# Modulation of a fused transformer kernel: feature-major tiles and one multiply-and-sum for each condition's column

## The reference

```python
for i in range(DEPTH):                       # 2 layers
    mx = (silu(c) @ w_mod[i] + b_mod[i]).reshape(B, 9, 1, D)     # for x
    mz = (silu(c_ctx) @ w_mod[i] + b_mod[i]).reshape(9, D)       # for z
    x = ffn_sublayer(x, mx, 0, ...)          # adaln_in(mod[0], mod[1]) ... gate mod[2]
    z = ffn_sublayer(z, mz, 0, ...)
    hx = adaln_in(x, g[2], mx[3], mx[4])     # rmsnorm(x, g) * (1 + scale) + shift
    yx = short_conv_mixer(hx, ...)           # layer 0; layer 1: window attention
    x = adaln_out(x, yx, g[3], mx[5], 1.0)   # x + weight * gate * rmsnorm(y, g)
    x = ffn_sublayer(x, mx, 6, ...)
```

## Time and profile before

| | us |
|---|---|
| median of 3 runs (2553.28 to 2557.42) | 2557.05 |
| the profiled execution, own time | 2558.84 |
| its span | 2557.5 |
| PE busy, 12614 matmuls | 2350.1 (92%) |
| DVE busy | 1600.0 (63%) |
| ACT busy | 900.6 (35%) |
| POOL busy | 176.5 (7%) |
| mean granted TensorE clock, share of 2.4 GHz | 0.925 |
| FFN 0, from its first matmul to its last | 60.85 to 450.88 |
| convolution | 483.00 to 672.39 |
| FFN 1 | 705.53 to 1096.01 |
| FFN 2 | 1128.12 to 1518.55 |

### The profile page before, as it was taken

The page is one execution under the profiler, slowest core; times in us unless marked ns, Lnnn a source line. Parts: engine busy times, 40 slices in busy tenths (PEclk is TensorE's granted clock), DMA queues, the critical chain, the costliest instruction groups (busy, mean ns, idle before and its releaser), DMA issues. The chain is left out here.

```text
span 2557.5 us, 32863 instructions
## 1 busy us (share of the span) xinstructions
PE 2350.1 (92%) x12614; PEld 1944.9 (76%) x12614; DVE 1600.0 (63%) x3977; ACT 900.6 (35%) x1542; POOL 176.5 (7%) x156
## 2 busy tenths in 40 slices
PE   5999999599699999959999987897997998999998
PEld 1788887488578888848888866577997975579998
DVE  6666668775676666876666685545455545445555
ACT  2322222422332222242222234455444444334444
POOL 2000001200300000120000022001002001001001
PEclk8999999799799999979999988898998996579999
DMA  7233434133123343413343332103556521014554
GB/s 275 99 120 144 152 133 155 58 148 114 74 99 144 133 160 123 149 74 133 127 153 148 124 140 87 42 25 113 177 179 211 184 86 50 1 67 149 182 173 140
DMA packets 62822, 322.45 MB, mean 126 GB/s; under 512 B 6446, under 2 KB 11182, under 8 KB 40778
## 3 DMA queue, kind: packets, MB, share of 16 engines
q1 hardware_dynamic: 60000, 314.33, 33.7%
q10 hardware_dynamic: 2666, 6.02, 0.7%
HBM read 319.27 MB, written 1.05 MB: 125 GB/s over the span
## 5 line engine op out<-in xcount | busy, mean ns | idle before, releaser
L418 PE MATMUL ps_g<-h,w_hi 128*128 128x512 f32 (+1 forms) x3360 | 963.1, 373 | 29.1 <-DVE h L788 28.7
L418 PEld LDWEIGHTS ps_g<-h,w_hi 128*128 128x128 f32 x3360 | 602.2, 191 | 150.5 <-DVE h L788 28.2
L746 DVE TENSOR_TENSOR w_lo<-w_raw,w_hi 128x1024 fp32r<-128x1024 f32 (+2 forms) x498 | 536.1, 1118 | 268.7 <-ACT w_hi L1187 267.1
L418 PE MATMUL ps_g<-h,w_lo 128*128 128x512 f32 (+1 forms) x1680 | 619.9, 369 | 0.0
L1187 ACT ACTIVATE w_hi<-w_raw 128x1024 fp32r<-128x1024 f32 (+2 forms) x498 | 455.4, 965 | 229.9 <-PE ps_g L418 202.9
L715 DVE SCALAR_TENSOR_TENSOR mod_acc<-mod_raw,cond,mod_acc 128x128 f32<-128x128 f32 x1792 | 489.3, 349 | 0.0
L418 PE MATMUL ps_g<-hid,w_hi 128*128 128x512 f32 (+1 forms) x1664 | 456.3, 362 | 1.5 <-DVE hid L944 0.9
L418 PEld LDWEIGHTS ps_g<-h,w_lo 128*128 128x128 f32 x1680 | 320.2, 191 | 56.5
L1272 ACT ACTIVATE gate_tmp<-ps_g 128x512 f32<-128x512 f32 (+1 forms) x118 | 61.1, 518 | 768.7 <-PE ps_g L418 768.7
L418 PEld LDWEIGHTS ps_g<-hid,w_hi 128*128 128x128 f32 x1664 | 293.3, 189 | 44.8 <-DVE hid L944 1.2
L418 PE MATMUL ps_g<-hid,w_lo 128*128 128x512 f32 (+1 forms) x832 | 298.3, 359 | 0.0
(11 more groups left out here) (235 smaller groups left out, 1986.6 us busy)
## 6 DMA issues: line engine op xcount, KB each, us to landing
w_raw<-in_gu SPq DMA_DIRECT2D x110, 1024.0 KB, 5.4
mod_raw<-in_w_mod SPq DMA_DIRECT2D x128, 512.0 KB, 3.4
w_raw<-in_conv_cu SPq DMA_DIRECT2D x8, 1024.0 KB, 5.5
w_raw<-in_w_in_a SPq DMA_DIRECT2D x8, 1024.0 KB, 4.7
w_raw<-in_w_in_d SPq DMA_DIRECT2D x8, 1024.0 KB, 4.8
w_mod<-in_w_mod SPq DMA_DIRECT2D x3, 2048.0 KB, 14.3
w_raw<-in_dn00a SPq DMA_DIRECT2D x8, 768.0 KB, 5.0
w_raw<-in_dn01a SPq DMA_DIRECT2D x8, 768.0 KB, 5.0
```

Of the source, the lines that this page charges most:

```text
L418: mm = pe.matmul(ps_g[:, 2 * (u % 2) + m, 0:T], w[wp][:, k, m * P:(m + 1) * P], acts[ap][:, k, 0:T], start=(k == 0 and n == 0), stop=(k == ...
L746: dve.tensor_tensor(w_lo[u % 2][:, cols], w_raw[u % 2][:, cols], w_hi[u % 2][:, cols].bitcast(F32), ALU.subtract).then_inc(lo_made, 1)
```

## The change

Tiles of w_mod are laid out with the 128 output features on the partitions and the 1024 inputs along the row. Both conditions, after silu, stand on every partition in a new tile `cond_b` (128 x 2 x 1024). For each condition, DVE multiplies the tile by the condition, sums along the row and adds the bias in one `tensor_tensor_reduce`, which leaves the finished column in `mod_sb`. Nothing is left for TensorE's partition sums and for `mod_keep`. The product itself is not needed: for the first condition it goes to PSUM (`dump`), for the second it overwrites the tile.

Ahead of unit 0 there are 16 tiles: eight scale tiles by TensorE in two groups of four, and eight shift tiles by DVE, from buffers of their own. The tiles on the way begin with 16 and belong to every unit of FFN 0, the convolution (now `conv_b` too), FFN 1 and the first 36 units of FFN 2. In the turn of u DVE makes tile MOD_OF[u] itself. `wide`, the input of the taps, has two buffers in place of eight, and the attention's scratch moves to other places.

```diff
-N_FIRST = 2 * NC + 1
+N_FIRST = 2 * NC
...
-MOD_OF = numbered(FFN_UNITS[0] + phase_units("conv_cu", "conv_out") + FFN_UNITS[1] + FFN_UNITS[2], N_FIRST)
-assert len(MOD_OF) + N_FIRST == N_MODS - 1
+MOD_OF = numbered((FFN_UNITS[0] + phase_units("conv_cu", "conv_b", "conv_out") + FFN_UNITS[1]
+                   + FFN_UNITS[2])[:N_MODS - N_FIRST], N_FIRST)
...
+    cond_b = sb("cond_b", [P, 2, D], F32, b1)
+    dump = ps_s[:, 2:4, :].rearrange("p a n -> p (a n)")
...
     def sync_program():
...
+        sp.dma_start(cond_b[:], t["cond"].partition_broadcast(P)).then_inc(cond_in, 16)
+        sp.dma_start(w_scale[0], t["w_scale"][0]).then_inc(scale_in[0], 16)
         sp.dma_start(x[:, :, 0:S], t["x"]).then_inc(x_in, 16)
+        shifts(0, 4)
         sp.dma_start(x[:, :, S:T2], t["ctx"]).then_inc(x_in, 16)
+        sp.dma_start(w_scale[1], t["w_scale"][1]).then_inc(scale_in[1], 16)
+        shifts(4, NC)
         for u, unit in enumerate(UNITS):
             if u >= 2:
                 sp.wait_ge(lo_made, 2 * (u - 2) + 2)
             sp.dma_start(w_raw[u % 2][:, 0:unit.elems], t[unit.src][unit.at]).then_inc(raw_in[u % 2], 16)
-            g = MOD_OF.get(u, 0)
...
-            if g > N_FIRST:
-                if g == N_FIRST + 1:
-                    sp.wait_ge(first_acc, STEPS * SUMMED)
-                else:
-                    sp.wait_ge(mod_step, STEPS * (g - N_FIRST - 1))
+            if u in MOD_OF:
+                g = MOD_OF[u]
+                if g >= N_FIRST + 2:
+                    sp.wait_ge(mod_step, 2 * (g - N_FIRST - 1))
                 sp.dma_start(mod_raw[g % 2][:], t["w_mod"][g]).then_inc(mod_in[g % 2], 16)
...
     def tensor_program():
         def feature_phase(name, acts, kc, mt, T, ready=None):
             for u in phase_units(name):
                 feature_unit(u, acts, kc, mt, T, ready if u == FIRST[name] else None)
-                if u in MOD_OF:
-                    mod_sum(MOD_OF[u])
...
     def vector_program():
+        def products(w, g, done, before):
+            for s in range(2):
+                if s == 0 and before:
+                    dve.wait_ge(done, before - 1)
+                dve.tensor_tensor_reduce(dump if s == 0 else w, w, cond_b[:, s, :], 1.0, b_mod[:, g, s:s + 1],
+                                         ALU.mult, ALU.add, mod_sb[:, g, s:s + 1]).then_inc(done, 1)
...
         def mod_products(g):
-            dve.wait_ge(mod_in[g % 2], ((g - N_FIRST - 1) // 2 + 1) * 16)
-            dve.wait_ge(mod_done, SUMMED + g - N_FIRST - 1)
-            accumulate(g % 2, mod_raw[g % 2][:], mod_step, STEPS * (g - N_FIRST))
+            n = g - N_FIRST
+            dve.wait_ge(mod_in[g % 2], 16 * (n // 2 + 1))
+            products(mod_raw[g % 2][:], g, mod_step, 2 * n)
...
-            if u in MOD_OF:
-                mod_keep(MOD_OF[u])
-                if not keep_off:
-                    mod_products(MOD_OF[u] + 1)
+            if u in MOD_OF and not keep_off:
+                mod_products(MOD_OF[u])
```

More of the change, by code:

```diff
@@ L133, in build @@
     tok = sb("tok", [P, 9])
-    mod_acc = sb("mod_acc", [P, 2, 2, P])
-    stats = mod_acc[:].rearrange("p a b n -> p (a b n)")[:, 0:5 * 64].rearrange("p (a n) -> p a n", n=64)
+    stats = sb("stats", [P, 5, 64])
     y = sb("y", [P, NC, T2])
-    mod_raw = [sb(f"mod_raw{j}", [P, NC, P]) for j in range(2)]
+    mod_raw = [sb(f"mod_raw{j}", [P, D]) for j in range(2)]
     mod_sb = sb("mod_sb", [P, N_MODS, 2])
@@ L146, in build @@
     h1 = [sb(f"h{j}", [P, NC, T2], F32R, b1) for j in range(2)]
[L147 removed]
+    wide = sb("wide", [P, 2, 2, S + 2], F32, b1)
+    cond_b = sb("cond_b", [P, 2, D], F32, b1)
     early1 = ExitStack()
[L149 to L150 removed]
+    w_scale = [y[:].rearrange("p a (b n) -> p (a b) n", n=P).rearrange("p (m k) n -> p m k n", m=4),
+               sb("w_scale", [P, 4, NC, P], F32, early1)[:]]
+    w_shift = sb("w_shift", [P, NC, D], F32, early1)
     early1.close()
+    apart = ExitStack()
+    sb("skip0", [P, NC, T2], F32, apart)
+    kv_raw = sb("kv_raw", [P, 8 * S], F32, apart)
+    sb("skip1", [P, NC, T2], F32, apart)
+    q_raw = sb("q_raw", [P, NC, S], F32, apart)
+    apart.close()
     hid1 = [sb(f"hid{j}", [P, FFN_HALVES[0], T2], F32R, b1) for j in range(2)]
@@ L282, in build @@
     stored = sem("stored")
-    w_mod_in = [sem(f"w_mod_in{j}") for j in range(6)]
+    cond_in = sem("cond_in")
+    scale_in = [sem(f"scale_in{j}") for j in range(2)]
+    shift_in = [sem(f"shift_in{j}") for j in range(NC)]
     raw_in = [sem(f"raw_in{j}") for j in range(2)]
@@ L364, in tensor_program @@
     def tensor_program():
[L365 to L373, removed]
         def first_mods():
@@ L720, in first_mods @@
             dve.wait_ge(consts_in, 48)
[L721 to L730, removed]
-                    w = w_mod[3][:, n] if n < 4 else mod_raw[0][:]
-                    accumulate(n % 2, w, first_acc, STEPS * n)
-                else:
-                    accumulate(n % 2, mod_raw[1][:], mod_step, 0)
-            dve.wait_ge(first_turned, 1)
-            dve.wait_ge(mod_done, SUMMED)
-            dve.tensor_tensor(mod_sb[:, 0:N_FIRST, :], ps_s[:, 2, 0:2 * N_FIRST].rearrange("p (m s) -> p m s", s=2),
-                              b_mod[:, 0:N_FIRST, :], ALU.add).then_inc(first_kept, 1)
-            dve.wait_ge(first_kept, 2)
+            dve.wait_ge(cond_made, 2)
+            for n in range(2):
+                for g in range(4 * n, 4 * n + 4):
+                    dve.wait_ge(shift_in[g], 16)
+                    products(w_shift[:, g, :], g, first_mod, 2 * g)
+                tiles = slice(NC + 4 * n, NC + 4 * n + 4)
+                dve.wait_ge(first_turned, n + 1)
+                dve.tensor_tensor(mod_sb[:, tiles, :], ps_g[:, 2 + n, 0:8].rearrange("p (m s) -> p m s", s=2),
+                                  b_mod[:, tiles, :], ALU.add).then_inc(first_kept, 1)
+            dve.wait_ge(first_kept, 3)
+            dve.wait_ge(first_mod, 2 * NC)
         def low_split(u):
@@ L1203, in first_mods @@
                            ACT.Silu).then_inc(cond_made, 1)
-            for n in range(3):
+            act.wait_ge(cond_in, 16)
+            act.activation(cond_b[:], cond_b[:], ACT.Silu).then_inc(cond_made, 1)
+            for n in range(2):
                 act.wait_ge(by_pe, n + 1)
-                act.activation(turn[0:2, n, :], ps_s[0:2, n % 2, :], ACT.Copy).then_inc(copied_by_pe, 1)
-                if n < 2:
+                act.activation(ring[n][0:2, :], ps_g[0:2, n, :], ACT.Copy).then_inc(copied_by_pe, 1)
+                if n == 0:
                     act.wait_ge(x_in, 32)
-                    for c in range(4 * n, 4 * n + 4):
+                    for c in range(NC):
                         square(sum_in(0), c, x[:, c, :], T2)
-                else:
-                    high_split(0)
-                    high_split(1)
+            high_split(0)
+            high_split(1)
             act.wait_ge(first_kept, 1)
```

100 lines of the change are left out of this document (31 added, 69 removed).

## The result

The changed kernel takes 2733.91 us (median of four runs, 2727.96 to 2739.45) where the kernel before takes 2555.75 beside it; the ratio is 1.0702, with a 95% interval of 1.0688 to 1.0715. It is slower by 7%. The forecast was 2720 with a range of 2640 to 2775. The profiled execution took 2727.96 (span 2726.6), which is the fastest of the four; the one of before took 2558.84.

A forecast was written before the change was run, and what follows sets the result against it. TensorE bounds the kernel before; after the change a one-turn loop through SP's wait would. FFNs +50, +54, +45, convolution +20, start -6 sum to +163 on 2558.84: 2722, taken as 2720 us, range 2640 to 2775.

The forecast's parts named there:

- The loop: SP's load, landing, split and products in one turn instead of two: 12.35 us per gu turn against TensorE's 11.15.
- The products: DVE's two new multiply-and-sums of 1024 columns per turn: 1.23 us a condition, 2.46 a turn.
- The upper bound of 2.9: Longest products per turn: two of 1225 ns, sum read not overlapped, 0.14 us each for writing the product.
- POOL's collision: In dn..b POOL's add falls on DVE's products and blocks them: 1.0 us added per turn.
- The convolution: Stage forecast from its loop turns: 209.8 us against 189.4, +20.
- FFN 0 and FFN 1: Stages slowed by the one-turn loop: +50 and +54 us, each with the later norm behind it.
- Ahead of unit 0: Start of the program, taken as bound by load arrivals: -6 us, between bounds of 2 and 10.
- The gaps: Behind FFN 0 and FFN 1 the norm starts 8.4 us later, as the last evacuation stands behind DVE's products.
- The one on the clock: Rival: TensorE's idling in dn..b drops its clock to 1.2 GHz, +74 us, 2795 in all; chance 0.08.
- The multiply-and-sum ran at full rate: Answers the rival of half rate with both operands in SBUF: 4.9 us a turn, 3005 in all; chance 0.04.
- The loop was not shorter than its rows: Answers the rival of a shorter loop that still binds: 2646 us; chance 0.10.
- The estimate from the Trainium skill: Tile and unit landing together as 2.0 us plus bytes over 436 GB/s: 5.6 us; sum 30 us lower.

## Why the prediction was right, and where it was off

**The loop** was the step that decided, and it holds: 12.35 us by the sum, 12.31 in the trace (median of 48 turns in gu); dn..a 10.5 and 10.38; a dn..a turn that splits a gu unit 11.75 and 11.66 to 11.98; dn..b with POOL 10.9 and 10.63; conv_cu 13.7 and 13.7; conv_b 12.9 and 12.9. Moving it a turn away gave back 238 us, and forcing it on the old kernel cost 436.

**The products** were put at 2.46 from rows with 512 and 256 columns and one operand in PSUM; they take 2.49 (114.59 to 117.08), the same with the product written to PSUM or to SBUF (1.29 and 1.28). The upper bound of 2.9 was not needed.

**POOL's collision** is there in dn..b, with 1.0 us. The product that it hits starts at 450.97 and takes 1.01 us longer, of the 1.21 that are left of POOL's add; the next is not slowed. By the Trainium skill, "SBUF — State Buffer", Summary: rules for kernel authors, a DVE operation with two SBUF inputs and a GpSimd one that reads SBUF block each other; the trace agrees. I had read this out of the earlier trace rows, where the operation of line 712 that is hit reads one tile and a column and not two tiles; only the rows after show it for two. In conv_out I counted one collision; there were two in two of its turns.

**The sizes that were off.** The convolution came out at +28.4, not +20.4. The term that was mis-sized is the end of it: I let the last unit start with its split, and did not see that the first unit of conv_out reads the last hidden tile, whose low half stands on DVE behind a split and therefore behind a landing. TensorE stops inside the unit (it began at 692.5):

```profile
706.48 1.22 PE L402 MATMUL ps_g<-hid,w_hi 128*128 128x512 f32 x2 [9.49 <-DVE hid L826]
...
702.92 2.36 DVE L709 TENSOR_TENSOR w_lo<-w_raw,w_hi 128x1024 fp32r<-128x1024 f32 x2 [5.80 <-ACT w_hi L1143]
705.20 1.22 DVE L826 TENSOR_TENSOR hid<-prod,hid 128x1024 fp32r<-128x1024 f32 x1
```

It then had the rest of that unit and three more to do at its own pace, to 748.79. With the hidden tile ahead of the split that wait of 9.49 is down to 1.41, and the convolution is 23.5 shorter.

FFN 0 and FFN 1 came out 4.6 and 2.8 us above the forecast (FFN 2 with its gap 2.5 below, as the dn..b turns were 0.3 shorter than my sum). Here it is the landing that was taken as constant. I used its median, and the median was right (5.46 to ACT's start in gu), but six of 59 there are 1.2 to 2.2 us late, and in the loop each of those is paid in full: 14 us in the three FFNs with those of the smaller units. One that took 7.1, in GB/s, the 8.5 us from 155 on in 40 slices; the second row is what came on the queue of instructions in the same 8.5 us (packets, MB, share):

```profile
GB/s 0 0 0 0 0 77 96 193 231 270 347 386 347 482 463 463 520 251 501 463 231 578 386 270 540 154 39 39 39 0 39 39 0 39 0 0 0 0 0 0
...
q8 instruction: 1, 0.02, 0.7%
...
w_raw<-in_gu SPq DMA_DIRECT2D x1, 1024.0 KB, 7.1
```

All but the last few packets are there after the usual time, and a tail of single packets (39 GB/s in a slice is one packet of 8 KB) comes up to 1.5 us later. The instruction queue brought one packet of 16 KB meanwhile, and that is the common case. In the FFNs of all ten traces, 123 of 137 late loads (over 0.8 us later than the median of their size) had such a packet beside them, and 113 of 983 of the others did; in the changed kernel they are 7 of 10 and 10 of 102 (112 of its 114 units there, all but the first two). So most late landings come with a fetch of instructions. How one packet holds up the others isn't shown, and three late loads of the changed kernel had none. With two turns of room a late landing costs nothing: the kernel before has 21, and its three FFNs take 390.0 to 390.5 us.

**Ahead of unit 0** it is -5.0 where I took -6. DVE's sixteen multiply-and-sums there end at 45.3. Five of them take 2.3 us instead of 1.3, while POOL adds. I had the arrivals as the bound. They were it only up to 31.09; from there the last eight run without a gap, so DVE and its collision with POOL set the end, which the forecast did not have. That the size came out near is in part luck. (The loads ran less evenly, too, than my 400 to 430 GB/s: the earlier trace rows have 347 to 378 in five slices.) The splits follow at 45.41 (50.42 before), and unit 0:

```profile
26.95 2.28 DVE L686 CUSTOM_DVE_ANT_0 w_shift<-w_shift,cond_b,vecs 128x1024 f32<-128x1024 f32 x1
...
45.41 4.63 DVE L709 TENSOR_TENSOR w_lo<-w_raw,w_hi 128x1024 fp32r<-128x1024 f32 x4
...
55.84 1.19 PE L402 MATMUL ps_g<-h,w_hi 128*128 128x512 f32 x2 [3.06 <-DVE h L746]
```

**The gaps** of +8.4 came out at +6.4 and +8.0: the last unit of dn0b was held up too, so the last addition (499.62 after a last matmul at 492.45) is 7.2 late and not 9.2. **The rest of the program** is 5.9 us shorter, 1000.9 against 1006.8. That is not told apart from the spread: in six other runs with the changed kernel's second block the same stretch takes 997.8 to 1005.1. No experiment was made on it.

**The rivals.** The one on the clock was partly true. Mean clocks of the FFNs are 0.96 to 0.97 against 1.00. This is where it goes (windows as above; the last row is of PE's timeline):

```profile
326.00:334.00 8.00, 8.00 (x36) 6.50 (x35) 1.31 (x3) 0.00 (x0) 0.00 (x0) 1.00 0.52 199
...
337.60:339.50 1.90, 1.87 (x4) 1.49 (x5) 1.90 (x4) 0.00 (x0) 0.00 (x0) 0.50 0.00 0
339.50:342.00 2.50, 2.50 (x10) 2.00 (x9) 1.69 (x3) 0.00 (x0) 0.00 (x0) 0.75 0.18 38
342.00:345.00 3.00, 3.00 (x15) 2.43 (x14) 0.00 (x0) 0.00 (x0) 0.00 (x0) 1.00 1.00 392
...
288.00:290.00 2.00, 2.00 (x9) 1.65 (x10) 2.00 (x3) 0.00 (x0) 0.00 (x0) 1.00 0.00 0
...
337.63 1.22 PE L402 MATMUL ps_g<-h,w_hi 128*128 128x512 f32 x2 [2.45 <-DVE w_lo L709]
```

TensorE works at 1.00 up to 335, waits 2.45 us for the split of unit 24, and resumes at 1.2 GHz (0.50); unit 24 takes 12.8 us in place of 11.4. After a wait of 3.1 us (284.9 to 288) it kept its clock. Fourteen units of the three FFNs are 1.3 to 2.6 us longer in this way, all behind a wait of 1.9 to 3.5 us, and six more are 0.8 to 2.0 longer behind a wait of 3.4 to 4.3 inside the unit ahead of them. The length of the wait alone doesn't tell: nine others of 1.7 to 3.1 us in the FFNs, and seven of 2.2 to 2.3 in the convolution, left the clock at 1.00. So my statement that no row shows a fall behind short gaps was right of the rows before, but the chip does it. The Trainium skill, "TensorE: Matmul & The Clock Gate", HAM oscillation — how this bites in real kernels, warns that waits repeated between groups of matmuls lower the clock. The trace agrees in that, but not every such wait did it. In FFN 0 eight units are longer in this way, by 13 us together. Little of it is paid, as TensorE is not the bound: the loop runs on beside a slow unit. Only the last unit of a stage is paid in full (1.5 us in dn0b). The 74 us of the rival did not come. The multiply-and-sum ran at full rate (1.29). The loop was not shorter than its rows (12.31). The estimate from the Trainium skill, "DMA: Bandwidth & Descriptors", Anatomy of one DMA — SWDGE (gpsimd) path (5.6 us from the tile's issue, by a fit for loads that GpSimd issues), was too small by 0.2 for these loads of SP: 0.37 and 5.4 to 5.46 were measured.

## What to carry to other kernels

When work is moved from one turn to the next, follow what its end releases: a queue in program order makes a load wait for anything that stands ahead of it, and a wait that had two turns of room becomes the period of the whole when it has one. Write that loop out, queue by queue, with the rows' durations, and compare its sum with the bound engine's period; here that sum was right to 0.05 us, and the saved work (15 us of TensorE per FFN, 62 of DVE) brought time only when the loop was gone. In such a loop a constant load time is the median at best, and its stragglers are paid each time.

## What the runs showed of the hardware

- Two loads of one queue issued 0.37 us apart don't share evenly: the unit (1 MB) lands in 4.8 us with 512 KB behind it, and in 5.4 with 512 KB ahead of it; the 512 KB take 3.3 as the first and 5.7 as the second.
- In the kernel before, 11 of 64 loads of 1 MB in the FFNs land over 0.8 us late, in the changed kernel 6, with the wait one tile tighter 15, with the unit ahead of the tile 1. Most late loads have a 16 KB packet of the instruction queue beside them (123 of 137 over all runs, and 113 of 983 of the loads that are not late).
- Behind waits of 1.9 to 4.3 us in the three FFNs of the changed kernel TensorE's clock fell to 1.2 GHz twenty times, for 4 to 13 matmuls each; sixteen other waits, of 1.7 to 3.1 us, left it at 2.4.
- A DVE multiply-and-sum of 128 x 1024 from two SBUF operands takes 1.29 us with its product to PSUM and 1.28 to SBUF, and the read of its sum adds hardly anything: a pair takes 2.49.
